# Column-grouped modulation between the latent projection's quarters, rotary chains for two heads, and the later modulation blocks in a buffer and a queue of their own

## The reference

```
mod = silu(c) @ w_ada + b_ada -> shift1, scale1, gate1, shift2, scale2, gate2
h   = RMSNorm(x) * (1 + scale1) + shift1
q_mla, ckv, kr, qkv_fox, f_logit, g_mla, g_fox = split(h @ w_in)
A: latent attention; q has 128 plain + 64 rotary features per head, 8 heads, one rotary key for all
B: forgetting attention, 8 heads of 128
merged = sigmoid(g_mla) * (o_mla @ w_o_mla) + sigmoid(g_fox) * (o_fox @ w_o_fox)
x = x + gate1 * (merged @ w_out)
x = x + gate2 * PEER(RMSNorm(x) * (1 + scale2) + shift2)     (16384 experts, 8 heads, top 16)
y = RMSNorm(x) * final_g
```

## Time and profile before

| | |
|---|---|
| median of 3 runs | 4213.12 us (4207.74 to 4215.14) |
| profiled execution, its own time | 4216.88 us |
| its span in the trace | 4215.1 us |
| mean granted TensorE clock | 0.901 of full |
| PE busy | 3431.2 us, 81% |
| DVE busy | 2839.5 us, 67% |
| POOL busy | 1448.8 us, 34% |
| ACT busy | 381.5 us, 9% |
| moved by DMA | 1412.71 MB, mean 335 GB/s |

### The profile page before, as it was taken

How to read it: one execution, slowest core, us unless ns; L and a number is a source line. 1 busy time by engine, 2 the same in 40 slices (tenths; PEclk the granted TensorE clock), 3 DMA queues, 4 the chain that set the end, 5 groups by cost and what they waited for, 6 DMA issues and landing times.

```text
span 4215.1 us, 39029 instructions
## 1 busy us (share of the span) xinstructions
PE 3431.2 (81%) x14249; PEld 2534.0 (60%) x14249; DVE 2839.5 (67%) x3456; ACT 381.5 (9%) x954; POOL 1448.8 (34%) x1094
## 2 busy tenths in 40 slices
PE   7899999999999999989987789999939999920000
PEld 5466678887845546567665567777727777720000
DVE  5354442237777876675676888886885555569998
ACT  0311110000211111110000011001000000010000
POOL 0000000000024543442444432323353566577764
PEclk9999999999999998989998899999969999965555
DMA  8577555567369998999999996889989999989997
GB/s 329 207 271 293 210 203 200 200 240 279 140 238 388 393 382 346 394 365 395 411 408 413 408 369 264 322 332 386 420 336 379 414 410 411 407 309 408 411 395 319
DMA packets 251314, 1412.71 MB, mean 335 GB/s; under 512 B 35312, under 2 KB 83456, under 8 KB 86144
## 3 DMA queue, kind: packets, MB, share of 16 engines
q0 software_dynamic: 124704, 841.18, 49.5%
q1 hardware_dynamic: 68832, 501.25, 30.4%
q10 hardware_dynamic: 57632, 68.41, 4.6%
HBM read 1359.60 MB, written 51.16 MB: 335 GB/s over the span
## 4 chain that ended last, share of the span: by engine, by line
PE 42%; DMA 23%; DVE 20%; POOL 7%; issue 4%; DVEq 2%; ACT 1%; PEld 0%; ACTq 0%; PEldq 0%; SPq 0%; POOLq 0%
PE pq L428 42%; DMA first<-peer_u,experts 10%; DMA first<-peer_v,experts 10%; DVE pq L1721 5%; POOL first L1879 4%; DVE late L1721 4%; DVE first L1711 3%; DMA ring<-wstream 2%; POOL got L1897 2%; DVE arena L1494 1%; DVE arena L1501 1%; POOL ring L1879 1%; DVE arena L1495 1%; DVE ring L1260 1%; PE pq L432 1%
## 5 line engine op out<-in xcount | busy, mean ns | idle before, releaser
L428 PE MATMUL pq<-h_last,ring 128*128 128x288 f32 (+2 forms) x6688 | 1669.6, 412 | 48.0 <-DVEq L1463 32.1
L428 PEld LDWEIGHTS pq<-h_last,ring 128*128 128x128 f32 (+2 forms) x6688 | 1270.2, 191 | 438.1 <-DVEq L1463 36.4
L1879 POOL DMA_INDIRECT first<-peer_u,experts x256 | 402.2, 1571 | 1721.8 <-DVEq L1556 1210.6
L1879 POOL DMA_INDIRECT first<-peer_v,experts x464 | 640.5, 1380 | 871.7 <-DVEq L1722 786.9
L1721 DVE SCALAR_TENSOR_TENSOR late<-first,wts,late 128x2048 f32<-128x2048 f32 x254 | 597.4, 2352 | 194.7 <-DMA first<-peer_v,experts 182.5
L1711 DVE CUSTOM_DVE_ANT_0 first<-first,late 128x2048 f32<-128x2048 f32 x256 | 582.9, 2292 | 212.2 <-DMA first<-peer_u,experts 203.5
L428 PE MATMUL pq<-first,ring 128*128 128x256 f32 (+2 forms) x3104 | 689.0, 384 | 11.1 <-DMA ring<-wstream 4.7
L428 PEld LDWEIGHTS pq<-first,ring 128*128 128x128 f32 (+2 forms) x3104 | 579.2, 188 | 114.8 <-issue 10.9
L1721 DVE SCALAR_TENSOR_TENSOR pq<-first,wts,pq 128x2048 f32<-128x2048 f32 x142 | 334.5, 2355 | 114.6 <-DMA first<-peer_v,experts 105.3
L1897 POOL DMA_INDIRECT got<-dots_dram,at_dot x288 | 325.2, 1129 | 105.7 <-issue 90.8
L428 PE MATMUL pq<-arena,ring 128*128 128x256 f32 (+2 forms) x1216 | 298.6, 407 | 49.0 <-issue 35.4
(11 more groups left out here) (197 smaller groups left out, 2054.2 us busy)
## 6 DMA issues: line engine op xcount, KB each, us to landing
ring<-wstream SPq DMA_DIRECT2D x478, 1024.0 KB, 7.7
dots_dram<-wts ACTq DMA_DIRECT2D x8, 2304.0 KB, 8.5
dots_dram<-stage ACTq DMA_DIRECT2D x128, 144.0 KB
first<-peer_v,experts POOLq DMA_INDIRECT x464, 11.4
got<-dots_dram,at_dot POOLq DMA_INDIRECT x288
first<-peer_u,experts POOLq DMA_INDIRECT x256, 9.9
out<-arena ACTq DMA_DIRECT2D x6, 512.0 KB, 6.4
o_last<-x_t ACTq DMA_DIRECT2D x5, 576.0 KB, 16.5
```

Source lines behind the costliest of these rows:

```text
L428: return nc.tensor.matmul(out, lhsT, rhs, start=start, stop=stop)
L1879: g.indirect_dma_start(out=slots[slot], out_offset=None, in_=peer_u if kind == "u" else peer_v, in_offset=bass.IndirectOffsetOnAxis(ap=exp ...
```

## The change

At the start all 32 blocks of shift1 and scale1 go to PE. silu(c) is padded to 32 columns, and the 16 products of one block go in turn to four groups of 32 PSUM partitions (four partial sums), each group with its own columns of the array. ACT copies four blocks' partial sums in one instruction, and PE sums the four groups while it turns rows into columns, by a matmul against the constant `stack`. The blocks come in the order that finishes shift and scale for two of the 16 feature blocks at a time, DVE makes their coefficients (`coef_step`), ACT normalizes four feature blocks at a time (`norm_step`), and each quarter of the latent projection (`token_chunk`) stands right behind the rows that it needs. x is loaded by SP ahead of the ring; small inputs and the rows of c for DVE are loaded later.

The rotary parts of two heads are projected together: block `r` has 128 columns, once in two heads, block `kn` has the keys' weights of two heads and is loaded only as wide as it is used (1024 columns). `rotate`, `keep_rope` and the scores use 64 partitions for each of the two.

The 64 later blocks leave the ring. POOL loads them one after the other to `fgb` (free until the final norm), each when DVE is done with the one before. DVE has one ahead of each head's maxima and one behind its `divide`, and two in each merge step; none are left in the `out` stage.

```diff
-for _i in range(ADA_A // 8):
-    for _k, _j in (("row", 0), ("row", 1), ("mod", 0), ("row", 2), ("row", 3), ("row", 4), ("mod", 1), ("row", 5)):
+for _i in range(2 * KC // 4):
+    for _b in (2 * _i, 2 * _i + 1, KC + 2 * _i, KC + 2 * _i + 1):
+        place(0, "row", 4 * _i + _b % 2 + 2 * (_b // KC), _b)
+    if _i >= 4:
+        place(0, "ckv", _i - 4, B_CKV + _i - 4)
...
         place(_g, "q", _h, B_MLA + 4 * _h + 2)
-        place(_g, "rkn", _h, B_MLA + 4 * _h + 3)
+        if _h % 2 == 0:
+            place(_g, "r", _h // 2, B_MLA + 4 * _h + 3)
+            place(_g, "kn", _h // 2, B_MLA + 4 * _h + 7)
...
+            for k in range(4):
+                for g in range(2):
+                    sp.dma_start(og[g][:, 4 * k:4 * k + 4, :], x_t[:, 4 * k:4 * k + 4, CG[g]:CG[g + 1]]).then_inc(x_in[k], 16)
...
                 for k in range(KC):
-                    last = mm(ps, cT[:, k, :], ring[:, n % RING, k * P:(k + 1) * P], k == 0, k == KC - 1)
+                    q = k % 4
+                    last = mm(ps[q * ADA_M:(q + 1) * ADA_M, :], cT[:, k, :], ring[:, n % RING, k * P:(k + 1) * P],
+                              k < 4, k >= KC - 4)
...
+            for i in range(ADA_A // 4):
+                if i >= 2:
+                    pe.wait_ge(row_ok, i - 1)
+                for j in range(4):
+                    ada_row(4 * i + j, pb[4 + i % 2][:, j * P:(j + 1) * P])
+                if i == 0:
+                    pe.wait_ge(cst_in, 16)
+                else:
+                    ada_cols(4, i, pb[6])
+                if i == 2:
+                    pe.wait_ge(sq_ok, 1)
+                    sumsq()
+                if i == ADA_A // 4 - 1:
+                    ada_cols(4, ADA_A // 4, pb[6])
+                if i >= 4:
+                    token_chunk(0, "ckv", 0, i - 4)
...
+            root(0, 0, T)
             for dst, src in ((g1T[:, :], g1), (g2T[:, :], g2), (kvgb[:, :], kvg.to_broadcast([P, LORA])),
...
+            for i in range(4):
+                for k in range(4 * i, 4 * i + 4):
+                    norm_step(k)
+                if i < 3:
+                    rows_trip(5 + i)
...
+            def mod_block():
+
+                i = mods_done[0]
+                idx = MODS[i][0]
+                mods_done[0] += 1
+                dve.wait_ge(mod_in, 16 * (i + 1))
+                v.tensor_tensor_reduce(out=g2b, in0=fgb[:, :], in1=crow[:, 0, :], scale=1.0, scalar=0.0,
                                        op0=ALU.mult, op1=ALU.add, accum_out=msum[:, 0, 0:1])
...
+                                       op0=ALU.mult, op1=ALU.add, accum_out=msum[:, 0, 1:2]).then_inc(mod_used, 1)
...
                     if g == 0:
-                        for q in range(2):
-                            mod_block(2 * KC + 2 * i + q)
-                    rotate(qr[:, 0:WG[g]], g, 9 * g + i + 2)
+                        mod_block()
+                    if i % 2 == 0:
+                        rotate([qr[:, 0:WG[g]]], g, RT * g + i // 2 + 2, 2 * ROPE)
                     fill(3)
                     row_max(g, head(g, i), cn["mask_mla"], SC_MLA)
                     fill(1)
                     divide(g, head(g, i))
+                    if g == 0:
+                        mod_block()
...
+            for i, (_, b) in enumerate(MODS):
+                if i > 0:
+                    pool.wait_ge(mod_used, i)
+                pool.dma_start(fgb[:, :], wstream[b]).then_inc(mod_in, 16)
```

More of the change, by code:

```diff
@@ L74 @@
 for _g in range(2):
-    for _c in range(CKV):
+    for _c in range(CKV * _g):
         place(_g, "ckv", _c, B_CKV + _c)
@@ L835, in _, with norm_step @@
             AFFINE = (((0, slice(0, WG[0]), 0),), ((1, slice(0, 2 * P), 0), (1, slice(2 * P, WG[1]), 1)))
+            def norm_step(k):
+                act.wait_ge(hn_ok, k + 1)
+                act.wait_ge(cf_ok, k // 2 + 1)
+                for g, cols, c in AFFINE[0] + AFFINE[1]:
+                    last = a(hg[g][:, k, cols], hg[g][:, k, cols], ACT.Identity, scale=cf[:, k, c:c + 1],
+                             bias=mod[:, k, c:c + 1])
+                last.then_inc(h_ok, 1)
             def norm(n, scale0, parts, coef):
@@ L1444, in mixers @@
                     if g == 0:
-                        for q in range(2):
-                            mod_block(3 * KC + 2 * i + q)
+                        mod_block()
                     row_max(g, head(g, i, True), cn["mask_fox"], 1.0)
@@ L1985 @@
         put(block(w_in[:, h * q_w:h * q_w + HD]))
-        put(pad(block(w_in[:, h * q_w + HD:(h + 1) * q_w]), block(ukv_h[:, h, 0])))
+        if h % 2 == 0:
+            put(block(np.concatenate([w_in[:, i * q_w + HD:(i + 1) * q_w] for i in (h, h + 1)], axis=1)))
+        else:
+            put(pad(block(ukv_h[:, h - 1, 0]), block(ukv_h[:, h, 0])))
     for c in range(2):
```

263 lines of the change are left out of this document (128 added, 135 removed).

## The result

| | us |
|---|---|
| kernel before, beside it (8 runs) | 4208.82 (4205.4 to 4215.14) |
| kernel after (8 runs) | 4231.05 (4220.0 to 4238.36) |
| ratio, 95% interval | 1.0048 (1.0034 to 1.0062) |
| profiled execution after, its own time | 4230.29, span 4228.5 |
| predicted | 4180, 4140 to 4228 |

The kernel is slower by 0.2 to 0.5%, where I had predicted 0.8% faster. The ratio of this one kernel differs by 0.3% between two chips, so ratios from different chips that differ by less are not held against each other. Stage lengths come from the traces, one execution each. The two profiled executions lie 13.4 us apart and the medians 22: the trace of the kernel before is of an execution 8 us above its median here.

A forecast was written before the change was run, and what follows sets the result against it. No single limit was taken, so each stage was read alone. Terms of -36.5 + 9 - 5 + 13 - 6.5 - 8 = -34 us against the profiled 4216.9 gave 4179 to 4183, stated as 4180; range 4140 to 4228.

The forecast's parts named there:

- start, to the first maxima: Start of the kernel: modulation blocks on PE in four column groups end it at 137 instead of 173.5, 36.5 us earlier.
- MLA of group 0: Group 0's latent attention heads: the chain of single-buffer loads loses 9 us and hides PE's saved 28.4; bounds -28, +24.
- FoX of group 0: Group 0's FoX heads: the chain of loads sums to 162.5 us against 167.2, a gain of 5; bounds -9, +12.
- merge: Group 0's merge steps: the load chain takes 22.0 us a step against PE's 20.9, 13 us lost; bounds 0, +65.
- `out`, to the first gather: Output stage: no modulation block left, so 16 units of 7.15 us, 6.5 us gained.
- behind the first gather: Group 1: PE, DMA and DVE have less to do, 8 us gained; bounds 0 and 20.
- my 1.8 us: Start: PE's time for one block with four column groups, between bounds of 0.9 and 3.65 us.
- a group of blocks is then 15.4 us: Start: time for each group of four blocks, DMA alone 12.7; three groups 46 us.
- the landing L: Later blocks: time from issue to landing of one load, 5.4 us on a quiet machine, bounded by 4.6 and 7.7.
- rival 2: Group 0's later blocks: the single buffer decides, with landings of 7.7 us, +90, 4270 us; chance 0.15.
- Rival 1: Start: the column groups follow one another, so it ends at 180 instead of 137, 4223 us; chance 0.15.
- Rival 3: Later blocks: the buffer is hidden, landings take 4.6 us, sum -73, 4143 us; chance 0.15.

The follow-up runs named there:

- clearing_later: The kernel after, with the writes that clear the table of dot products moved from group 0's MLA heads to behind the merge; 4201.03 us, ratio 0.9967 to before.
- two_buffers: The kernel after, with a second buffer for the later modulation blocks; 4166.02 us, ratio 0.9884 to the kernel before.
- one_column_group: The kernel after, with all 16 products of a modulation block in one column group instead of four; 4257.06 us, ratio 1.0090 to the kernel before.
- the mends: The kernel after with two buffers, small loads issued first and clearing writes behind the merge; 4150.34 us, ratio 0.9859 to the kernel before.
- after_again: The kernel after, unchanged, run again on another chip; 4220.84 us, ratio 1.0020 to the kernel before.

## Why the prediction was wrong

The terms of my sum beside the same stretches of the two traces, in us. Each measured term reaches from one landmark to the next, so that they add up to the 13.4 us between the spans:

| | predicted | measured |
|---|---|---|
| start, to the first maxima | -36.5 | -12.0 |
| MLA of group 0 | +9 | +23.8 |
| between MLA and FoX | 0 | +1.5 |
| FoX of group 0 | -5 | -1.2 |
| merge | +13 | +6.9 |
| `out`, to the first gather | -6.5 | -7.5 |
| behind the first gather | -8 | +1.9 |
| sum | -34 | +13.4 |

Two steps failed most: the start, by 24.5 us, and group 0's MLA, by 15, together 39 of the 47 us between forecast and trace. With the start right alone the trace would have been some 11 us faster than the one before, with MLA right alone as good as even. Two of my own signs of being wrong were on record. One came true (the start ends later than 150: 160.5), the other did not (mixers and merge together lose more than 45: they lost 31).

**Start: -36.5 predicted, -13 at the end of the latent projection.** The opening was near: the first block was worked at 24.1 (21.5 predicted), 20 blocks by 73.6 (71), one each 2.6 us on average. The column groups were better than my 1.8 us: a block takes 1.08 us at a granted clock of 1.00 and mostly 1.93 at 0.50. What failed are two other terms. "The first coefficients come near 76": they came at 84.2. The krT load was issued at 63.6 and not by 61, and took 20.6 us and not the 14.9 of the earlier trace rows; the first quarter ended at 99.1 and not 88. And "a group of blocks is then 15.4 us": it was 20.0 to 21.0. I had added work and DMA time, but not the slot of the ring that the quarter holds (2.0 to 3.5 us of waiting for the fourth block). The normalization between the turn and the quarter I had put at nothing, and TensorE waited 2.06 us for it. The quarter I had taken at full clock, 7.2 us for 9.0 to 9.9. The three groups made 61.1 us where I had 46 + 2.5. Small loads first and the later quarters together bring the end to 150.5 and 149.2 us; what is left to 137 stays open.

**MLA of group 0: +9 predicted, +23.8 measured.** The chain was the right one (free, issue, landing, 4.5 us, once more), and the traces show which of its terms were too small. One is the landing L: I had 6.4 us from even to odd head and 7.05 + 6.2 from odd to even, from ring blocks of before, whose wait has other blocks in it. The loads that VectorE waited for took 5.1 to 9.8 us, in both heads of a pair: +9.4 us over the stage. The other is "rotation and scores 3.7": from the rotation to the maxima it was 5.2 to 5.3 us, with TensorE at a granted clock of 0.50 (247.0 to 252.3 us): +4.7 over three times. That is 14.1 of the 15. The intervals were 18.7 to 23.0 and 29.4 to 29.7 us in place of 19.6 and 26.7. With the landing of 5.1 us of `clearing_later` my formula gives 18.3 us from even to odd head, and that kernel shows 18.2 to 18.7. I had named the clearing in rival 2 ("clearing the dots table") and given that rival 0.15. Taking the writes away takes the whole loss away.

**FoX -5, merge +13, out -6.5.** Measured -1.2, +6.9 (from the last FoX maxima to the output stage, 349.5 us instead of 342.6) and -7.5. They add up to -1.8 where I had +1.5, but that is luck, since neither FoX nor the merge went as I had worked it out. In FoX the loads landed in 5.1 us, where I had 6.0; the six short intervals were 5 us less in sum than mine, and the one with the value projection was 45.4 us and not 36.5. In the merge a landing took 5.3 us, where I had 6.1. My chain is then 2 x (4.9 + 5.3) = 20.4 us a step, shorter than PE's 20.9, and nothing should be lost. Indeed PE worked its 16 steps in 334.8 us without a wait for a block, 1.0 more than before. The loss stands at one place, which I had put at nothing, the end of the stage. The last sum of the merge stands on VectorE behind a block that lands late, and TensorE waits for it ahead of `out`, 7.7 us where it was 2.1 (VectorE first, then TensorE):

```profile
940.00 2.29 DVE L1303 CUSTOM_DVE_ANT_0 late<-fgb,late 128x2048 f32<-128x2048 f32 x1 [7.05 <-DMA fgb<-wstream]
...
945.73 0.42 DVE L1504 TENSOR_TENSOR arena<-arena 128x256 f32<-128x256 f32 x1
```

```profile
946.28 4.18 PE L437 MATMUL pq<-arena,ring 128*128 128x256 f32 x9 [7.71 <-issue]
```

In `two_buffers` this wait is 2.1 us again.

**Group 1: -8 predicted, +5.4 measured in MLA** (+4.7 to +11.6 over the traces with the same order). I had asked only what PE and VectorE have less to do, not where the pair's rotation stands: behind five dot products that wait for gathers, on an engine that is busy 78% of the stage. FoX then gave 4.5 us back, within what that stage varies by.

**Rivals.** Rival 1 is refuted by `one_column_group`, although its 4223 lies nearer to the measured 4231 than my 4180; with one group the start ends at 192.9 us and the time is 4257. Rival 2 named the right wait but the wrong measure: not the median landing (5.3 us over all 64, where it asked for 7.5) decided, but the ones beside the clearing. Rival 3, the buffer hidden, is what two buffers do, and 4143 was its time; that kernel took 4166, and 4150 with the mends. The Trainium skill's estimate of 4.4 us for such a load (DMA: Bandwidth & Descriptors, Anatomy of one DMA) stayed below the shortest landing here, 4.9.

## What to carry to other kernels

When a prefetch through a shared queue is replaced by one buffer, price the chain free, issue, land, use as the new bound, and price the landing beside the traffic of that very stage; a second buffer is worth the search for its memory. An instruction that releases another engine must not stand in a queue behind one that waits for a load: look at what every merged or moved step stands behind, on each engine. A saving on an engine counts only where this engine's row, in the stage's window, is full. A stage whose total comes out right can still have been worked out wrongly: hold every step of the sum against its own rows.

## What was not expected of the hardware

- Four column groups ran 3.8 times as fast as one (0.94 us a block against 3.54 in the windows shown), close to four.
- A load of 32 KB on ScalarE's queue, issued at 63.6 us behind weights in flight, landed 20.6 us later.
- Where TensorE stood still for a larger part of a stage its granted clock was lower: in the start TensorE was busy 76% and granted 0.90 before, 60% and 0.78 after; in MLA of group 0 96% and 0.99 before, 71% and 0.83 after, 94% and 1.00 with two buffers. Part of what TensorE saves is so given back where it must wait: the quarters of the latent projection took 9.0 to 9.9 us, where four in a row had taken 30.1. A modulation block took 1.08 us at the 2.4 GHz level (granted 1.00) and 1.93 at the 1.2 GHz level (0.50). The first three blocks, from 24.1 us, took 1.93 to 1.94 us too, although the record shows 1.00 for them; why stays open.
- What follows the first gather took between 2996 and 3018 us in the traces of this study, although hardly anything there was changed. The kernel after itself has 3006 and 3018 in its two traces. The runs of one kernel scatter by as much (4209 to 4240 us in `after_again`), so a gain of some us ahead of the gather is seen in the stage and not in one time.
